# Last expert layer: two narrow units transposed at once in seven places, and expert 0's tokens gathered token tile by token tile

## What is computed

```python
N_EXPERTS_2, D_FF, TOP_K = 8, 3584, 2
xt = _rms_norm(x, norm_g).reshape(-1, d)                # 256 tokens x 1024
logits = xt @ w_router
top_vals, top_idx = lax.top_k(logits, TOP_K)
gates = jax.nn.softmax(top_vals, axis=-1)
...                                                     # for each expert e, for its tokens xb:
(jax.nn.silu(xb @ w_gate[e]) * (xb @ w_up[e])) @ w_down[e]
...                                                     # times the gate, added to x
```

## Time and profile before

| what | value |
|---|---|
| median of 3 runs | 2046.38 us (2045.41 to 2047.74) |
| the profiled execution | 2042.38 us, its span 2040.5 us |
| busy in the span | PE 1865.1 us (91%), PEld 949.6 us, DVE 745.9 us, ACT 295.1 us, POOL 58.0 us |
| weight DMAs of the last layer after its first nine | 159, issued from 1231.74 us on |
| first unit of the last layer starts on PE | 1223.55 us |

### The profile page before, as it was taken

One profiled execution on the slowest core, in us unless ns is written; L12 is line 12 of the kernel. 1 busy time (PEld: TensorE's weight loads), 2 busy tenths in 40 slices (PEclk: granted clock), 3 DMA queues, 4 the chain that ended last, 5 costly groups with the idle time before them and its releaser, 6 DMA issues.

```text
span 2040.5 us, 29153 instructions
## 1 busy us (share of the span) xinstructions
PE 1865.1 (91%) x12658; PEld 949.6 (47%) x12658; DVE 745.9 (37%) x1429; ACT 295.1 (14%) x533; POOL 58.0 (3%) x39
## 2 busy tenths in 40 slices
PE   9998976676567799999999999999999999999998
PEld 6787642222222256577777664443333433333332
DVE  4486543333333358335668631111010211122112
ACT  3243221111111116201010030000000000000000
POOL 0026000000000000000000000000000000000000
PEclk9999988878887799999999999999999999999999
DMA  7201489999999961353534358999999999999995
GB/s 282 95 7 45 185 375 430 430 431 430 430 430 430 425 268 42 144 233 128 202 150 181 125 207 354 431 403 399 430 431 431 431 430 429 430 430 431 431 430 251
DMA packets 51685, 646.62 MB, mean 317 GB/s; under 512 B 8288, under 2 KB 10592, under 8 KB 12768
## 3 DMA queue, kind: packets, MB, share of 16 engines
q1 hardware_dynamic: 51552, 644.68, 75.3%
HBM read 643.61 MB, written 1.05 MB: 316 GB/s over the span
## 4 chain that ended last, share of the span: by engine, by line
PE 84%; DMA 8%; DVE 4%; issue 3%; ACT 1%; SPq 0%; DVEq 0%; POOL 0%; ACTq 0%; POOLq 0%
PE low L961 41%; PE high L961 40%; DMA slot<-in_moe_w_up 8%; PE low L1721 1%; DVE hact L2811 1%; PE high L1237 1%; DVE sg L2811 0%; DVE MQ L2811 0%; PE low L975 0%; DVE x_sb L2818 0%; PE low L1840 0%; PE high L1169 0%; DVE hT L2811 0%; ACT slot L2303 0%; PE high L1840 0%
## 5 line engine op out<-in xcount | busy, mean ns | idle before, releaser
L961 PE MATMUL high<-slot,hTs 128*64 128x512 f32 (+2 forms) x1232 | 253.6, 596 | 0.9 <-DVE hTs L3442 0.9
L961 PE MATMUL low<-slot,hT 128*64 128x512 f32 (+1 forms) x848 | 246.0, 596 | 0.7 <-DVE x_sb L2818 0.6
L961 PE MATMUL high<-slot,xgT 128*32 128x512 f32 (+1 forms) x1216 | 191.3, 640 | 24.6 <-issue 15.3
L961 PE MATMUL low<-hT,slot 128*128 128x256 f32 (+1 forms) x1008 | 209.9, 370 | 0.5 <-DVE hT L2811 0.5
L961 PE MATMUL low<-slot,xgT 128*32 128x512 f32 (+2 forms) x848 | 177.1, 688 | 35.7 <-issue 23.2
L961 PEld LDWEIGHTS low<-hT,slot 128*128 128x128 f32 x1008 | 184.0, 190 | 27.2 <-issue 3.3
L961 PEld LDWEIGHTS high<-slot,hTs 128*64 128x64 f32 (+2 forms) x1232 | 80.3, 132 | 166.8 <-issue 166.8
L961 PEld LDWEIGHTS low<-slot,xgT 128*32 128x32 f32 (+2 forms) x848 | 57.2, 143 | 144.1 <-issue 138.3
L961 PEld LDWEIGHTS low<-slot,hT 128*64 128x64 f32 (+1 forms) x848 | 78.1, 143 | 98.6 <-issue 94.8
L961 PEld LDWEIGHTS high<-slot,xgT 128*32 128x32 f32 (+1 forms) x1216 | 55.3, 121 | 136.0 <-issue 121.9
L3442 DVE COPY hTs<-low 128x256 f32<-128x256 f32 x35 | 14.8, 424 | 243.9 <-PE low L1721 243.9
(11 more groups left out here) (490 smaller groups left out, 1999.2 us busy)
## 6 DMA issues: line engine op xcount, KB each, us to landing
slot<-in_moe_w_down SPq DMA_DIRECT2D x88, 2048.0 KB, 21.6
slot<-in_moe_w_up SPq DMA_DIRECT2D x88, 2048.0 KB, 22.5
slot<-in_moe_w_gate SPq DMA_DIRECT2D x69, 2048.0 KB, 18.6
tables<-in_moe_w_gate SPq DMA_DIRECT2D x19, 2048.0 KB, 19.5
slot<-in_dffn_w_down SPq DMA_DIRECT2D x7, 2048.0 KB, 7.4
slot<-in_dffn_w_gate SPq DMA_DIRECT2D x7, 2048.0 KB, 7.5
slot<-in_dffn_w_up SPq DMA_DIRECT2D x7, 2048.0 KB, 12.1
slot<-in_w_in_tiles SPq DMA_DIRECT2D x6, 2048.0 KB, 8.5
```

Of the source, the lines that this page charges most:

```text
L961: return nc.tensor.matmul(o, l, r, start=start, stop=stop)
```

## The change

Two edits to the last expert layer.

*Pairs.* In seven places, units (0,1), (4,5), (7,8), (10,11), (14,15), (19,20) and (22,23), two narrow units of one expert that follow each other put their activations into one tile `hsb_two`: the first in partitions 0 to 63, the second in 64 to 127. PE transposes neither in the step after the first; in the step after the second it transposes both at once with four 128x128 transposes, DVE copies them in one piece to `hT_two`, and PE does both down products in that step, the first unit's before the second's. Both new tiles lie in columns of `tables` that were constants of earlier layers.

*Gather by token tile.* Expert 0's tokens of the first token tile are ranked by a matmul of their own and gathered on their own, without the `keep_busy` matmuls, into another bank than those of the second tile; DVE adds the two parts (`gather_fixed`, `places_fixed`). `in_order` moves behind that.

```diff
+                self.pair_of, n = {}, 0
+                while n < self.at[WIDE - 2, 0] - 2:
+                    (k, c), (k2, c2) = self.seq[n:n + 2]
+                    if k == k2 and not self.wide(k):
+                        self.pair_of[n], self.pair_of[n + 1] = n, n
+                        n += 1
+                    n += 1
...
+            def turned_at(self, n):
+
+                return n + 2 if self.first_of_two(n) else n + 1
...
+            def downs(self, n):
+
+                return [u for u in (n - 2, n - 1) if 0 <= u and self.turned_at(u) == n]
...
-                    if n:
+                    if n - 1 in m.downs(n):
                         turn_hidden(n - 1)
                     if n < UNITS:
                         hidden(n, 1)
-                    if n:
-                        down_proj(n - 1)
+                    for u in m.downs(n):
+                        down_proj(u)
...
+            def gather_fixed():
+
+                m = mix2
+                for t in range(TT):
+                    pe.wait_ge(normed, TT * NORMS.index("moe") + t + 1)
+                    pe.wait_ge(m.fixed_chosen, t + 1)
+                    for q in range(KT):
+                        o = psum[4 + q // 4 if t else 7]
+                        last = mm(o[:, q * HALF:q * HALF + HALF], xn[:, t, q * P:q * P + P], selh[:, t, 0:HALF])
+                        if q == KT - 1 or t and q == KT // 2 - 1:
+                            last.then_inc(m.fixed_gathered, 1)
...
-                keep_busy(psum[7], 1)
+                if x is moe1:
+                    keep_busy(psum[7], 1)
...
+                        rows_ = slice(HALF, P) if n in m.pair_of and not m.first_of_two(n) else slice(0, HALF)
+                        dst = hsb_two if n in m.pair_of else hsb
+                        tt(dst[rows_, :], b[HALF:CAP, :], sgx[0:HALF, :], ALU.mult).then_inc(ring.emptied, 1)
...
+            def places_fixed():
+
+                by_block = lambda x: x.rearrange("p (q c) -> p q c", c=HALF)
+                dve.wait_ge(mix2.fixed_gathered, 1)
+                do(tt(xgh[:, :, :], by_block(psum[7]), spread(pcol("moe", 0, KT), HALF), ALU.mult))
+                for h in range(2):
+                    q, cols = slice(4 * h, 4 * h + 4), slice(4 * h * HALF, 4 * h * HALF + 4 * HALF)
+                    dve.wait_ge(mix2.fixed_gathered, h + 2)
+                    do(tt(by_block(hsb[:, cols]), by_block(psum[4 + h][:, cols]), spread(pcol("moe", 4 * h, 4), HALF),
+                          ALU.mult))
+                    ins = tt(xgh[:, q, :], xgh[:, q, :], by_block(hsb[:, cols]), ALU.add)
+                ins.then_inc(mix2.fixed_placed, 1)
...
-            counts = V.take(dve, V.at["count2"])
-            in_order(counts)
-            ranks(moe2, V.at["rank2"])
-            for k in mix2.gathers(-1):
-                choose_mixed(k)
-            rooms(counts)
+            dve.wait_ge(mix2.tile_ranked, 1)
+            first = cnt8[:, 0, 0:1]
+            do(stt_(first, psum[6][:, FIXED:FIXED + 1], 1.0, msk[:, 0, FIXED:FIXED + 1], ALU.add, ALU.mult))
+            choose_fixed(0, 0, first).then_inc(mix2.fixed_chosen, 1)
+            counted_places(moe2, V.at["rank2"])
+            choose_fixed(1, 0, rank[:, 1, FIXED:FIXED + 1]).then_inc(mix2.fixed_chosen, 1)
+            rooms(V.take(dve, V.at["count2"]))
             enough_room()
-            for k in mix2.gathers(-1):
-                places_mixed(k)
+            places_fixed()
+            in_order()
```

More of the change, by code:

```diff
@@ L647, in __init__ @@
                 self.at = {u: n for n, u in enumerate(self.seq)}
-                self.chosen = sorted([k for k in range(N_E2) if k not in group[1:]], key=self.first)
+                self.pair_of, n = {}, 0
[5 more added lines that the diff above has]
+                    n += 1
+                self.tile_ranked, self.fixed_chosen = sem("mixed_tile_ranked"), sem("mixed_fixed_chosen")
+                self.fixed_gathered, self.fixed_placed = sem("mixed_fixed_gathered"), sem("mixed_fixed_placed")
+                self.chosen = sorted([k for k in range(LAST) if k not in group[1:]], key=self.first)
                 stages = []
-                for k in self.gathers(-1):
-                    stages.append((("x", k), self.banks_of(k)))
                 for n in range(UNITS + 1):
-                    if n:
+                    if n and self.turned_at(n - 1) == n:
                         stages.append((("hT", n - 1), 1))
@@ L677, in gathers @@
             def gathers(self, n):
-                return [k for k in self.chosen if k not in group and max(self.first(k) - 2, -1) == n]
+                return [k for k in self.chosen if k not in group and self.first(k) - 2 == n]
             def parts(self, n):
@@ L1504, in dense @@
                 if x is moe2:
-                    mix2.ring.landed(pe, mix2.ring.at["x", LAST])
+                    pe.wait_ge(mix2.fixed_placed, 1)
                 for t in range(TT):
@@ L1668, in hidden @@
                     xg = m.gathered(k)
-                    if part == 0 and c == 0 and k not in group:
+                    if part == 0 and (k, c) == (LAST, 0):
+                        pe.wait_ge(m.fixed_placed, 1)
+                    elif part == 0 and c == 0 and k not in group:
                         ring.landed(pe, ring.at["x", k] + m.banks_of(k) - 1)
@@ L1939, in experts @@
                 pe.wait_ge(chosen_two, seen + 1)
+                if x is moe2:
+                    S_.landed(pe, x.last_s)
+                    mm(psum[6][:, 0:n], cst("before"), msk[:, 0, 0:n]).then_inc(mix2.tile_ranked, 1)
                 mm(b[:, 0:n], cst("before"), msk[:, 0, 0:n])
@@ L3705, in ranks @@
                 dve.sem_inc(V.emptied, 1)
+            def ranks(x, item):
+                n = x.count
+                counted_places(x, item)
                 do(ts(rank[:, :, 0:n], rank[:, :, 0:n], -1.0, ALU.add))
@@ L4220, in _ @@
             two_of(2, 8, 1)
-            counts = V.take(dve, V.at["count2"])
-            in_order(counts)
-            ranks(moe2, V.at["rank2"])
-            for k in mix2.gathers(-1):
-                choose_mixed(k)
-            rooms(counts)
-            enough_room()
-            for k in mix2.gathers(-1):
-                places_mixed(k)
+            dve.wait_ge(mix2.tile_ranked, 1)
[5 more added lines that the diff above has]
+            rooms(V.take(dve, V.at["count2"]))
+            enough_room()
+            places_fixed()
+            in_order()
+            for t in range(TT):
+                own(choose_fixed(t, 1, rank[:, t, FIXED:FIXED + 1]))
+            own.settle()
+            do(ts(rank[:, :, 0:N_E2], rank[:, :, 0:N_E2], -1.0, ALU.add))
             by_order(rank, rank_o)
```

72 lines of the change are left out of this document (37 added, 35 removed).

## The result

| | before | after |
|---|---|---|
| median of 16 runs of each | 2045.26 us | 2050.61 us |
| lowest and highest run | 2041.31, 2051.64 | 2048.47, 2053.39 |
| span of the profiled execution | 2040.5 us | 2047.8 us |
| PE starts on unit 0 | 1223.55 | 1226.01 |
| gate tile of unit 3 issued | 1231.74 | 1236.65 |

What follows compares the result with a forecast made beforehand. PE was taken to set the time, with the queues 0.2 us ahead at unit 55. Start -1.3, hole +3.2, reserve -0.2 gave +1.7, 2044.1 us; the median lies 4.0 above, so 2048.1, range 2043.3 to 2051.7.

Steps and rivals of the forecast that it cites:

- The mechanism of the queues: Weight queues: unit 10's down tile waits for unit 7's delayed down product, queues run empty, end 0.8 to 2.9 us later.
- the sign of the start: Start of the last layer: unit 0 begins at 1222.3 instead of 1223.55, 1.3 us earlier, for queues and PE both.
- the wide one: Range of the predicted median, 2043.3 to 2051.7 us, meant to leave out no more than 2 in 10.
- the rival that came true: The clock stays down through the gather: unit 0 starts 1.4 to 3.2 us later, sum +4.4 to +6.2 us; 17%.
- 9 instructions: Expert 0's gather: instructions run at the lower clock from 1216.3 to about 1218.5, at 0.24 us each.
- the other 23: Expert 0's gather: the remaining instructions run at the upper clock, taking 2.8 us and ending at 1221.3.
- of a gain as long as the clock comes back as it did: Start of the layer: unit 0 1.3 us earlier, or 2.7 us earlier with the upper clock throughout.
- The hole of pair (7,8): Queues before unit 10's down tile, issued at 1363.7 instead of 1349.5: +3.2 us, net of the old holes.
- the 7.3 and 9.4 that bounded it: Issue to landing with an empty queue, in us; puts unit 10's down tile at 1371.0 to 1373.1.
- 2 to 3 us: Total of PE's waits for weight tiles expected somewhere in units 51 to 55, where it waited for none.
- The pairs on PE: Transposes of seven pairs: 0.26 us saved each, 1.8 us in all, worth nothing unless the queues gain too.
- The reserve of 0.2 us: Unit 55: its up tile lands at 2011.5, PE starts at 2011.65; queues later by more than that move the end.

Runs made afterwards that it cites:

- f1: The kernel before without the eight keep_busy instructions of the last layer's start, nothing else changed; median 2047.91 us, ratio 1.0019.
- e5: The changed kernel with unit 10's down tile issued behind gate and up of unit 12, and the eight keep_busy instructions back; median 2044.98 us, ratio 0.9999.
- g1: e5's kernel measured again, on the same chip as g2; median 2044.39 us, ratio 1.0003.
- e2: The gather by token tile alone, every unit transposed by itself, against the kernel before; median 2047.49 us, ratio 1.0007.
- e4: The changed kernel, but SP issues the down tile of unit 10 behind gate and up of unit 12; median 2046.41 us, ratio 1.0004.
- p1: The kernel before profiled once more, with the same code; one run, 2049.65 us.
- e1: The kernel before with the seven pairs alone, the start of the layer as it was; median 2049.78 us, ratio 1.0022.
- e3: The kernel before with six pairs, units 7 and 8 transposed apart, and the old start; median 2045.33 us, ratio 1.0003.
- e6: The kernel before with the seven pairs, and unit 10's down tile issued behind gate and up of unit 12; median 2042.48 us, ratio 0.9993.
- g2: e6's kernel measured again, on the same chip as g1; median 2042.59 us, ratio 0.9996.
- f2: As e5, with twelve keep_busy instructions ahead of the gather where e5 has six; median 2045.65 us, ratio 1.0002.
- e7: As e6, but for every pair the down tile waiting for its first down product goes behind the next unit's gate and up; median 2043.18 us, ratio 0.9997.

## Why the prediction was right, and where it was not

The measured median, 2050.61, lies in the range and 2.5 us above the predicted 2048.1; the change was slower, by the 0.2% that was my bound, where I had called no change the likeliest. The mechanism of the queues was right, and the sign of the start was wrong.

That the number came so near is luck. It lies outside the forecast's own range, 2047.0 to 2049.1, and inside the wide one only because that made room for the rival that came true. The profile was missed by 5.5 us (2049.61 for 2044.1), and 3.0 of that was made up by a second miss: I had added 4.0 us from the profiled execution to the median, and in the changed kernel it is 1.0.

**The start: wrong.** The step that failed is the gather of "9 instructions" at the lower level and "the other 23" at the upper one, and behind it the bounds "of a gain as long as the clock comes back as it did". All 32 ran at the lower one, 7.07 / 32 = 0.22 us each, and so did unit 0. The start became 20.52 - 16.65 = 3.9 us longer, not 1.3 us shorter; 1.0 us more of the 4.9 lies ahead of the last mask, where nothing was changed (0.3 us already at 1209, 0.7 in the router's products at the lower clock). I had written this case down as a rival with 17%, its gather at 7.7 us and its sum at +4.4 to +6.2 (measured +7.3 in the profile, 5.35 in the medians). I gave it so little because the gather of the earlier trace rows had not brought the clock down. That was the wrong question. What matters is what had brought it up, and the runs point at the eight `keep_busy` instructions, which the change removes: f1 removes them alone and has the lower clock and 1.0019; e5 and g1 put them back, and in their profiles the clock is back before unit 0. In the four profiles without them (after, e2, e4, f1) the gather never saw the upper clock, in the ten with them it did eight times. The rule that I cited from the Trainium skill ("TensorE: Matmul & The Clock Gate", section "Part 1: The HAM clock gate"), that the throttled clock is the default and activity releases it, described this better than my reading of one profile. The trace agrees so far: in the changed kernel 7 us of weight loads with 64 columns each left the clock at 0.50. It does not tell the whole, since in p1 and e1 the clock stayed at 0.50 behind all eight `keep_busy` instructions as well.

**What the start is worth by parts.** At the lower clock the new order is shorter than the old one without `keep_busy` by 22.94 - 20.47 = 2.5 us (f1 against the mean of after and e2; with e4, whose clock fell later, it would be 2.7). That is the gain that the edit was able to give, in the profiles. The `keep_busy` instructions that it leaves out are worth 22.94 - 17.3 = 5.6 us when they bring the clock back (17.3 is the mean of the five old starts in which they did). The edit trades 5.6 us, in five profiles of seven, for 2.5. The timed runs agree in direction: f1's median is 3.7 us above the kernel before, e2's 2.2, the latter within the noise.

**The fall of the clock** is not the change's. It was at 0.50 more than 1 us ahead of the last mask in p1, e3, e6, g2 and f1, all with the old order, as it was in the changed kernel, in e2 and f2, and it fell within half a microsecond of it in the first profile of before and in e1, e4, e5, e7 and g1; and p1 shows that the kernel before can lose 7 us in the same place. The prediction compared with one profile, a favourable one: it is 2.9 us below the median of 16 runs, that of the changed kernel 1.0. That is the difference between the 7.3 us of the profiles and the 5.35 of the medians.

**The hole of pair (7,8): right in place, smaller in size.** Predicted was +3.2 - 0.2 = 3.0 us net; the rest of the span grew by 2.4 (after) and 2.2 (e1). e3 takes the one pair out and the loss is gone, e4 takes the blocking out and it is gone. The tile was issued 132.4 us behind the first issue, and landed 7.9 us later, between the 7.3 and 9.4 that bounded it. Two details were off. I had the queues stand empty for 5 us ahead of that issue; all tiles had landed only 0.9 us before (1368.2), because the pair (4,5) had made its own hole, at 1320, of which I had said that (7,8) closes it. It left the queues 3.7 us late (the up tile of unit 11 lands 131.5 us behind the first issue, for 127.8 before), so it took that much from the hole of (7,8). By itself it costs nothing at the end: e3 has it alone, and its rest is below that of the kernel before. And "2 to 3 us" of waits for weight tiles was the loss, not what PE would show: 5.0 us, the loss plus the time that PE itself had gained.

**The pairs on PE: the condition right, the size too small.** 1.8 us were predicted as PE's gain, worth nothing unless the queues gain too. e6 has 3.3 us of it at unit 55. 0.6 us of that is a wait for DVE (on `x_sb`, the second of the two of the earlier trace rows) that is gone; 2.7 are left for my 1.8. Up to unit 10 the timelines of before and e6 give it pair by pair, at the next instructions that both have: 0.3 us for (0,1), 0.7 each for (4,5) and (7,8), where I had 0.26. I had counted the transposes' own durations alone. At (4,5), from start to start, the step without transposes is 0.44 us shorter and the transposes of the other step are 0.05 longer, but both halves of the wide product and the two down products together are some 0.1 shorter each as well; no run says why.

At the end 2.1 us of it are seen. With the tile put off the rest is 806.4 to 806.9 in seven profiles, for 808.3 to 809.0 in the four of kernels without pairs. But in all seven PE waits 1.1 to 1.8 us for the up tile of unit 55. What reaches the end is what the queues have gained, because PE frees the slot of unit 14's gate tile sooner, and that has the condition of the prediction on its side: PE's time counts where the queues gain with it.

**The reserve of 0.2 us: right**, as far as it can be read: the landings at unit 14 and at unit 55 are late by the same 7.4 us, and the span by 7.3.

**What stays open.** Why the clock comes back in some executions of one program and not in others, and when it falls: no run here separates that. And whether the version with the old start and the tile put off beats the kernel before: both its profiles say that its part behind the first issue is about 2.1 us shorter, pooled medians say 2 us (2042.48 for 2044.6), the intervals of both measurements contain 1.

## What to carry to other kernels

Instructions that only keep an engine busy are not idle work to be traded for an earlier start: look at what the clock does with and without them, in more than one profile, and whether they stand in a gap that another engine makes anyway. Where one in-order queue issues all transfers, a step that delays one buffer's release delays everything behind it in that order; before such a step is moved, list which of the following transfers have free buffers, and move the late one behind them. When such a queue and an engine are nearly even, read the two accounts apart (time at the first transfer, and the rest), since waits of the engine add up the loss of one and the gain of the other. And after a repair ask again which of the two sets the end: a time saved on the engine may count only through the buffer that it frees sooner.

## What the runs showed of the hardware that I had not expected

- The same program had its granted clock at 0.50 from about 1215.3 to 1218.7 in one profile and from about 1213.4 to 1233.8 in another (p1): 6.8 us of difference in one small part of 2040.
- The lower clock stretched the gather (32 instructions, 64 columns) from 3.7 to 7.1 us, a factor of 1.9, so these loads of 128x128 weights (3.65 us in all in the first profile, 6.95 in that of the changed kernel) follow the clock as the products do.
- A tile of 2 MB issued to queues that have just run empty landed 7.3 us (unit 3's gate tile, before) to 9.4 us later (unit 14's), while in full queues one lands every 4.9 us: by my estimate an empty queue costs 2.4 to 4.5 us on top of the time it is empty.
